# Attention of the first block by pairs of heads, in ten passes a layer instead of 28

## The reference, cut to what matters

```python
proj = h @ w_in                                   # q, k, v (24 heads x 64) and 3 x 1024 gate columns
gates = jax.nn.sigmoid(proj[..., 3 * MIX_WIDTH:]).reshape(B, S, N_BRANCHES, D)
o_a = dilated_mixture(q[:, a_sl], k[:, a_sl], v[:, a_sl])      # 12 heads, 3 groups of 4, merged by logsumexp
o_b = moba_attention(q[:, b_sl], k[:, b_sl], v[:, b_sl])       # 6 heads, one block: causal softmax
o_c = stick_breaking_attention(q[:, c_sl], k[:, c_sl], v[:, c_sl])   # 6 heads, suffix sums of log_sigmoid
y_a = flat(o_a) @ w_out_a                         # likewise y_b, y_c
merged = gates[:, :, 0] * y_a + gates[:, :, 1] * y_b + gates[:, :, 2] * y_c
x = x + merged @ w_o
```

## Time and profile before

| | |
|---|---|
| median of 3 runs | 1539.34 us (1539.24 to 1539.76) |
| span of the profiled execution | 1537.9 us |
| median less span | 1.4 us |
| attention stage of layer 0 (first scores to first `out` product) | 120.05 to 253.60, 133.55 us |
| attention stage of layer 1 | 604.20 to 737.24, 133.04 us |
| first merge by DVE to last, layer 0 | 256.09 to 282.71 us |
| busy in the span | PE 97%, DVE 60%, ACT 52% |

### The profile page before, as it was taken

One profiled execution on the slowest core, in us unless ns is written; L12 is line 12 of the kernel. 1 busy time (PEld: TensorE's weight loads), 2 busy tenths in 40 slices (PEclk: granted clock), 3 DMA queues, 4 the chain that ended last, 5 costly groups with the idle time before them and its releaser, 6 DMA issues.

```text
span 1537.9 us, 21514 instructions
## 1 busy us (share of the span) xinstructions
PE 1484.8 (97%) x8288; PEld 1195.1 (78%) x8288; DVE 918.7 (60%) x1687; ACT 793.9 (52%) x1349; POOL 91.4 (6%) x142
## 2 busy tenths in 40 slices
PE   7999998999999999998999999999999899999998
PEld 6887777799887787877789978787776348788776
DVE  4554456766554554455866666677544874669655
ACT  5445786355534445687445554434565302344774
POOL 6050000000000000000000000000000000041220
PEclk9999999999999999999999999999999999999999
DMA  8782334788554754232489654462222001164200
GB/s 275 253 184 83 125 122 164 219 224 215 192 191 164 276 198 155 83 122 98 171 242 261 191 192 165 164 165 68 71 83 74 22 0 39 45 178 134 81 29 29
DMA packets 183701, 220.96 MB, mean 144 GB/s; under 512 B 6619, under 2 KB 103429, under 8 KB 183600
## 3 DMA queue, kind: packets, MB, share of 16 engines
q1 hardware_dynamic: 179376, 211.65, 43.5%
q0 software_dynamic: 3184, 7.93, 2.6%
q10 hardware_dynamic: 1040, 0.00, 0.0%
HBM read 216.55 MB, written 3.01 MB: 143 GB/s over the span
## 4 chain that ended last, share of the span: by engine, by line
PE 78%; DVE 13%; ACT 6%; issue 3%; DMA 0%; DVEq 0%; SPq 0%; ACTq 0%
PE bank L620 21%; PE bank L622 21%; PE bank L621 21%; DVE w_low L1793 2%; PE bank L1107 2%; ACT w_high L1357 1%; PE bank L863 1%; PE bank L1070 1%; PE bank L704 1%; PE bank L807 1%; PE bank L1083 1%; PE bank L838 1%; PE bank L637 1%; PE bank L812 1%; DVE arena L2150 1%
## 5 line engine op out<-in xcount | busy, mean ns | idle before, releaser
L1793 DVE TENSOR_TENSOR w_low<-raw,w_high 128x1024 fp32r<-128x1024 f32 x344 | 414.9, 1213 | 340.8 <-ACT w_high L1357 335.7
L1357 ACT ACTIVATE w_high<-raw 128x1024 fp32r<-128x1024 f32 x352 | 367.0, 1047 | 334.8 <-PE bank L622 284.8
L620 PE MATMUL bank<-w_high,acts_r 128*128 128x512 f32 (+1 forms) x848 | 339.0, 400 | 11.6 <-DVE w_low L1793 4.9
L621 PE MATMUL bank<-w_low,acts_r 128*128 128x512 f32 (+1 forms) x848 | 329.7, 389 | 0.0
L622 PE MATMUL bank<-w_high,acts_r 128*128 128x512 f32 (+1 forms) x848 | 329.7, 389 | 0.0
L620 PE MATMUL bank<-acts_r,w_high 128*128 128x256 f32 (+1 forms) x736 | 228.9, 311 | 1.5 <-DVE arena L2209 1.3
L622 PE MATMUL bank<-acts_r,w_low 128*128 128x256 f32 (+1 forms) x736 | 225.6, 307 | 0.0
L621 PE MATMUL bank<-acts_r,w_high 128*128 128x256 f32 (+1 forms) x736 | 225.6, 307 | 0.0
L620 PEld LDWEIGHTS bank<-w_high,acts_r 128*128 128x128 f32 x848 | 160.2, 189 | 53.5 <-DVE w_low L1793 6.6
L622 PEld LDWEIGHTS bank<-w_high,acts_r 128*128 128x128 f32 x848 | 159.4, 188 | 36.4
L621 PEld LDWEIGHTS bank<-w_low,acts_r 128*128 128x128 f32 x848 | 159.8, 188 | 32.0
(11 more groups left out here) (315 smaller groups left out, 1789.6 us busy)
## 6 DMA issues: line engine op xcount, KB each, us to landing
raw<-in_w_in SPq DMA_DIRECT2D x69, 1024.0 KB, 5.2
raw<-in_w_up SPq DMA_DIRECT2D x64, 512.0 KB, 6.7
raw<-in_w_down SPq DMA_DIRECT2D x32, 1024.0 KB, 4.9
raw<-in_w_ada SPq DMA_DIRECT2D x24, 1024.0 KB, 6.9
raw<-in_w_in SPq DMA_DIRECT2D x34, 512.0 KB, 5.1
raw<-in_w_o SPq DMA_DIRECT2D x8, 1024.0 KB, 7.6
raw<-in_w_out SPq DMA_DIRECT2D x8, 1024.0 KB, 4.9
raw<-in_w_out_c SPq DMA_DIRECT2D x4, 768.0 KB, 5.3
```

Source lines behind the costliest of these rows:

```text
L620: mm(o, lh, rh, start=start, stop=False)
L621: mm(o, lh, rl, start=False, stop=False)
L1357: run(A_(high, src, ACT.Copy), (high_ready, n + 1))
L1793: run(V.tensor_tensor(low, src, high.bitcast(F32), ALU.subtract), split_done(n))
```

## The change

A unit becomes a pair of heads: A has 2 pairs x 2 tiles, B 3 pairs with both query tiles, C 3 pairs, so ten units, and PE does pass i as `scores(i)`, `second(i - 1)`, `steps_of` filler steps (8, 9, 8, 9, then 10 three times, 9 three times, the last five at the end), `values(i - 1)`. The two heads of a pair alternate: scores on row halves 0 to 63 and 64 to 127, each in its own bank; values with v stationary on column halves, so that the output comes by features and 128 probabilities' columns move. The sums' inverses are spread over the features by a matmul, as in block 2; ACT copies that to `spread1` and DVE multiplies it into `o_feat`. The 16 transposes are gone; `oT` is split per branch, A and B inside the passes (`take_heads_high`, `take_heads_low`). The copy of a gate group by ACT is replaced by a minimum on DVE (`gate_floor`), for which ACT's Abs waits; the four ACT steps of a group are no longer spread over passes. Half of the copies to `PT` go to DVE. The filler's order in a slab is by two k for each tile (`by_tile`).

On PE:

```diff
-                for u in range(len(U) + 2):
-                    if u < len(U):
-                        scores(u)
-                    if 1 <= u <= len(U):
-                        second(u - 1)
-                    advance(filler, 1000 if u >= len(U) else 3 if U[u][0] == "A" else 4)
-                    if u >= 2:
-                        values(u - 2)
-                for b in range(4):
-                    o = open_bank("oT", l, b)
-                    for m in range(4):
-                        ins = tr(o[:, m * P:(m + 1) * P], o_tok[:, t, k * P:(k + 1) * P], ident[:, :])
+                steps_of = {"A": (8, 9), "B": (10,), "C": (9,)}
+                for i in range(len(U) + 1):
+                    if i < len(U):
+                        scores(i)
+                    if i:
+                        second(i - 1)
+                    advance(filler, steps_of[U[i][0]][U[i][2]] if i < len(U) else 1000)
+                    if i:
+                        values(i - 1)
...
+                def scores(i):
+                    if kind == "A" and t:
+                        third = open_bank("s2", l, i, among=ATTENTION_BANKS)
+                        ins = mm(third[:, SEQ:2 * SEQ], head(0, hd, slice(P, SEQ)), head(1, hd, keys), start=True, stop=True)
+                    o = [open_bank("s", l, i, side, among=ATTENTION_BANKS) for side in range(2)]
+                    if kind == "A":
+                        for g in range(G_A - t):
+                            for side in range(2):
+                                ins = mm(o[side][:, g * span:(g + 1) * span], head(0, hd, slice(t * P, (t + 1) * P)),
+                                         head(1, hd, slice(0, span)), start=True, stop=True)
+                        if t:
+                            pe.wait_ge(*third_scored.at(l, i))
+                            ins = mm(third[:, 0:SEQ], head(0, hd, slice(P, SEQ)), head(1, hd, keys), start=True, stop=True)
...
+                def second(i):
+                    for side in range(2):
+                        pe.wait_ge(*probs_ready.at(l, i, side))
+                        o = open_bank("p", l, i, side, among=ATTENTION_BANKS)
+                        for b in range(min(4, blocks)):
+                            ins = tr(o[:, b * P:(b + 1) * P], S[:, i % 2, side, b * P:(b + 1) * P], ident[:, :])
+                    if blocks > 4:
+                        o = open_bank("p", l, i, 2, among=ATTENTION_BANKS)
+                        for side in range(2):
+                            for b in range(4, blocks):
+                                ins = tr(o[:, at_b:at_b + P], S[:, i % 2, side, b * P:(b + 1) * P], ident[:, :])
...
+                    half = [o[side * DH:(side + 1) * DH, :] for side in range(2)]
+                        for b in range(blocks):
+                            for side in range(2):
+                                mm(half[side][:, 0:P], v(g * N_A + 2 * p + side, jt), PT[side][:, b * P:(b + 1) * P],
+                                   start=b == 0, stop=b == blocks - 1)
+                    if kind != "C":
+                        for tt in range(n):
+                            for side in range(2):
+                                inverse = stat[:, (2 * i + side) % 4, 3, tt:tt + 1].to_broadcast([P, DH])
+                                ins = mm(half[side][:, (n + tt) * P:(n + tt + 1) * P], inverse, ident[:, :], start=True, stop=True)
```

On ACT:

```diff
+                def gate_log_steps(key):
+                    splits.due(*key)
+                    if n >= 2:
+                        act.wait_ge(*gate_exponent.at(l, n - 2))
+                    act.wait_ge(*gate_floored.at(l, n))
+                    run(A_(x, bank(*key)[:, :], ACT.Abs, scale=nstat[:, 2, t:t + 1]), emptied(*key))
+                    run(A_(x, x, ACT.Exp, scale=-1.0))
+                    run(A_(x, x, ACT.Ln, bias=eps_col[:, 1:2]), gate_logged.by(l, n))
+                for i in range(len(U) + 1):
+                    if i >= 2:
+                        take_sums(i - 2)
+                    if i:
+                        take_second(i - 1)
+                    if i < len(U):
+                        exponents_of(i)
+                        splits.due("s", l, i, 1)
+                    while len(done) < len(logged):
+                        gate_exp_step()
+                    if i in (6, 9):
+                        take_heads_high((6, 9).index(i))
+                    for key in ended_in[(l, i)]:
+                        gate_log_steps(key)
+                splits.due("o", l, len(U) - 1)
+                take_sums(len(U) - 1)
+                take_heads_high(2)
+                while len(done) < len(logged):
+                    gate_exp_step()
```

On DVE:

```diff
+                def gate_floor(key):
+                    splits.due(*key)
+                    dve.wait_ge(*filled(*key))
+                    run(V.tensor_scalar(g, bank(*key)[:, :], nstat[:, 2, t:t + 1], 0.0, ALU.mult, ALU.min), gate_floored.by(l, len(floored) - 1))
+                for i in range(len(U) + 1):
+                    if i:
+                        invert_sums(i - 1)
+                    early = i >= 2 and U[i - 2][0] == "A"
+                    if early:
+                        take_values(i - 2)
+                    if i < len(U):
+                        maximum(i)
+                    if i >= 2 and not early:
+                        take_values(i - 2)
+                    if i:
+                        take_second(i - 1)
+                    gate_exponents()
+                    if i in (7, 10):
+                        take_heads_low((7, 10).index(i))
+                    if i < len(U):
+                        splits.due("s", l, i, 1)
+                        stick_sums(i)
+                    for key in ended_in[(l, i)]:
+                        gate_floor(key)
+                splits.due("o", l, len(U) - 1)
+                take_heads_low(2)
+                gate_exponents()
```

More of the change, by code:

```diff
@@ L658, in tokens_by_features @@
                 order = [(k, t) for k in range(KD) for t in tiles]
+                if by_tile:
+                    order = [(k, t) for k0 in range(0, KD, 2) for t in tiles for k in (k0, k0 + 1)]
                 if apart:
@@ L798, in scores @@
                     if kind == "A":
                         span = (t + 1) * P
[L800 to L807, removed]
@@ L1428, in take_second @@
                     if kind == "C":
[L1430 to L1431 removed]
+                        for side in range(2):
+                            act.wait_ge(*emptied("p", l, i, side))
+                            run(A_(PT[side][:, 0:384], S[:, i % 2, side, 384:768], ACT.Exp), stick_weights.by(l, i, side))
                         return
[L1433 removed]
@@ new lines, in exponents_of @@
+                def exponents_of(i):
+                    kind, p, t = U[i]
+                    for side in range(2):
+                        st = stat[:, (2 * i + side) % 4, :, :]
+                        s = S[:, i % 2, side, :]
+                        if kind == "C":
+                            act.wait_ge(*emptied("s", l, i, side))
+                            part = s[:, 384:768]
+                            run(A_(part, s[:, 0:384], ACT.Abs))
+                            run.settle()
+                            run(A_(part, part, ACT.Exp, scale=-1.0))
+                            run.settle()
+                            run(A_(part, part, ACT.Ln, bias=eps_col[:, 1:2]), softplus_part.by(l, i, side))
+                            continue
+                        act.wait_ge(*bias_ready.at(l, i))
+                        if kind == "A":
+                            w = blocks_of_pair(kind, t) * P
+                            run(A_(s[:, 0:w], s[:, 0:w], ACT.Exp, bias=st[:, 1, 0:1], scale=SCALE, accum_out=st[:, 2, 0:1]),
+                                probs_ready.by(l, i, side))
+                        else:
+                            for tt in range(TILES):
+                                x = s[:, tt * P:tt * P + (tt + 1) * P]
+                                run(A_(x, x, ACT.Exp, bias=st[:, 1, tt:tt + 1], scale=SCALE, accum_out=st[:, 2, tt:tt + 1]),
+                                    probs_ready.by(l, i, side) if tt else None)
@@ L1509, in _ @@
-                while len(done) < len(copied):
-                    if len(logs) < len(copied):
-                        gate_log_step()
-                    gate_exp_step()
-                for b in range(4):
-                    splits.due("oT", l, b)
-                    act.wait_ge(*filled("oT", l, b))
-                    take_high(A_(oT[:, 0, 2 * b:2 * b + 2, :], bank("oT", l, b)[:, :].rearrange("p (a n) -> p a n", a=2), ACT.Copy),
-                              "oT", l, b)
+                    run(A_(logged[n], logged[n], ACT.Exp), gates_ready.by(l, n))
```

428 lines of the change are left out of this document (209 added, 219 removed).

## The result

The changed kernel takes 1549.14 us (1548.01 to 1549.54), against 1539.76 us for the kernel before in the same series: ratio 1.0057, 95% interval 1.0044 to 1.0071. (Ratios are taken over all fast executions of both kernels and so aren't the quotient of the two medians.) The forecast was 1552.5. So it is slower, a little less than forecast, and that the size came so near is luck: layer 0 lost 10.0 us and layer 1 lost 1.35, where 6.6 each was forecast, and the two errors nearly cancel.

A forecast was written before the change was run, and what follows sets the result against it. PE's order of work bounds the kernel, except where PE stands behind DVE. Tail 3.4 and clock 3.2 us, twice, add 13.2 to the span of 1537.9: 1551.1, plus 1.4 to the median: 1552.5 us; range 1520 to 1566.

The forecast's parts named there:

- PE's work: Attention stage: PE relieved of 21 us a layer, 104 left; a pair of 256-column scores takes 0.45 to 0.50 us.
- that rival: Scores: row halves do not overlap, costing 11.5 us more a layer; 1560 to 1575 us, chance 0.06.
- ACT and DVE: Attention stage: ACT about 86 us, DVE about 80, neither a bound by its sum; order within a pass counts.
- the mechanism that the prediction named: Gate passes: DVE does low parts, then minima; ACT waits for the minimum before 2 x 2.05 us of logarithms.
- Waits in the passes: Attention passes worked: PE waits 26 us in a layer, nearly all of the 21 us given back.
- The clock: Half clock after idle gaps: two losses of 1.6 us a layer, 3.2; bounds none and four (6.4).
- the prediction's use of it: Skill's clock rule: waits of passes 2, 4, 5 and 10 each lose clock, 6.4 us a layer, giving 1558.9.
- the prediction's one place of agreement: Earlier trace: after windows with PE busy 1.46 of 3 us, the clock was 0.50 for the next 3 us.
- The term of +3.4: Tail behind the last gate: first merge at 142.3 against 136.04, DVE done 3.4 us later, same in both layers.
- first merge some 10 us behind the first `out` product: Sign in the trace after, start of `out`: first merge some 10 us behind PE's first product instead of 2.5.
- Neither half nor all of the gain: Rival, PE stays the bound, faster: all waits vanish, 1494 us, or half, 1520; together 0.24, full gain a third.
- No change: Rival: with 3.4 us less a layer and no clock loss the stage comes out even, 1536.3 to 1542.4; 0.13.

The follow-up runs named there:

- e6_copy: Changed kernel with layer 0's conditioning steps moved into pass 1, ACT copying gate groups again and the minimum back in DVE's last step: 1515.14 us.
- e7_all: Changed kernel with conditioning early, minima ahead of low parts, high parts ahead of exponentials and gate logarithms a pass later: 1496.31 us.
- e1_cond: Changed kernel with DVE's three conditioning instructions of layer 0 moved from behind the last gate exponents into pass 1: 1539.82 us.
- e2_floor: Changed kernel with conditioning early, and DVE's gate minima ahead of the low parts due with the gate's bank: 1522.47 us.
- e10_copy_only: Changed kernel with only DVE's minimum undone: ACT copies the gate group again, conditioning stays late: 1530.79 us.
- e5_by_side: Changed kernel with a pair's scores not alternating, all of side 0 and then all of side 1: 1553.74 us.

## Why the prediction was right, and where it wasn't

**PE's work: right.** Six scores of 256 columns in row halves start at 153.03 and the transposes at 154.53: 1.50, so 0.50 for a pair, the upper end of what was taken.

```profile
153.03 0.48 PE L814 MATMUL bank<-arena 64*128 64x256 f32 x1
...
154.53 0.87 PE L866 MATMUL bank<-ident,arena 128*128 128x128 f32 x6
```

Row halves do overlap (before, three heads took that time); that rival falls. The third groups, which the forecast had standing alone (1.95 for the six), overlap with the others too. Values took 1.36 for 24 records, 0.11 a matmul, a spread 0.32. In sum 103.96 us were measured where PE had its full clock, against 104 predicted.

**ACT and DVE: right.** ACT 89.0 and DVE 73.9 us in layer 0 (predicted 86 and 80), 81.7 and 69.1 in layer 1, none a bound by its sum. DVE's minimum takes 0.745 us (predicted 0.68):

```profile
L2076 DVE TENSOR_SCALAR arena<-bank,nstat 128x512 f32<-128x512 f32 x12 | 8.4, 745 | 0.0
```
```profile
L1527 ACT ACTIVATE arena<-bank,nstat 128x512 f32<-128x512 f32 x12 | 8.1, 678 | 15.0 <-DVE arena L2076 15.0
```

ACT stood 15.0 us behind it, the mechanism that the prediction named and e6_copy confirms.

**Waits in the passes: right in place, too large.** By hand against measured: pass 2 4.4 and 3.66, pass 3 0.9 and 0.67, pass 4 3.65 and 3.04, pass 5 5.4 and 4.1, pass 6 1.6 and 0.7, pass 8 5.6 and 3.6, pass 10 4.2 and 1.2; 26 and 17 in sum.

**The clock: right in kind, too small.** The passes began at 8.3, 18.1, 33.9, 44.5, 60.2, 74.8, 85.7, 94.8, 109.8 and 120.1, near to the hand's, though the waits are 9 us shorter. PE's own work makes up the rest. It is busy 112.61 us, 8.65 more than at full clock in e7_all; 1.7 of it in the conditioning matmuls, 7 in the passes, where the forecast had 3.2 and 6.4 as its bound. So the clock's term was some 4 us too small, and the waits 9 us too large. Pass 2, timeline of PE:

```profile
142.84 1.11 PE L873 MATMUL bank<-ident,arena 128*128 128x128 f32 x4 [3.66 <-DVE arena L2060]
143.60 0.78 PE L629 MATMUL bank<-w_high,acts_r 128*128 128x512 f32 x1
...
147.59 0.57 PE L629 MATMUL bank<-w_high,acts_r 128*128 128x512 f32 x1
```

Nine products take 3.99 us, 0.42 to 0.58 each, instead of 0.23. The same pass takes 15.8 us here and 9.6 without the wait in e7_all: a wait of 3.66 cost 6.2 (in layer 1, where the pass takes 15.0, it cost 5.4). So taking waits away can bring more than their sum. For e6_copy it can be counted: from e1_cond the stage up to the first `out` product shrank from 129.88 to 117.61 us, 7.5 of it the listed waits (19.6 to 12.1), 4.8 PE's busy time (110.16 to 105.39). The Trainium skill (TensorE: Matmul & The Clock Gate, HAM oscillation) has this loss behind longer idle gaps. By the prediction's use of it, 6.4 a layer, the size is nearly right. Its places were not: half clock followed the waits of passes 2 and 4 and the wait of 1.8 us at the end of pass 8, and not those of pass 5 (2.1 and 2.0) and 10 (1.2). A fall behind 1.8 us is not what that section has, and the measurement decides. Nor was the prediction's one place of agreement a longer gap: PE stood there 1.12, 0.94 and 0.92 us, with work between.

**The step that failed: the tail of layer 0.** The prediction took layer 0 and layer 1 as equal ("Layer 1 has the same order, +3.4"). It had listed DVE's order behind the last gate and left out its three steps on `cond`, which stand in the program behind `gate_exponents()` in layer 0 alone, and for which PE's conditioning product waits, ahead of `out`. Before, DVE had done them 1.0 us ahead of PE's product, and they cost nothing, but the trace before has both rows (DVE, then PE):

```profile
250.48 0.18 DVE L2009 TENSOR_TENSOR cond<-cond,cond_e 128x16 f32<-128x16 f32 x1
```
```profile
251.67 1.92 PE L704 MATMUL bank<-raw,cond 128*32 128x512 f32 x16
```

The term of +3.4 for layer 0's last merge, +6.6 with the clock, was +10.0; e1_cond puts 8 to 9 us on this wait. With it the sign "first merge some 10 us behind the first `out` product" failed in layer 0 (3.6 us; 8.3 in layer 1). Layer 1's +6.6 was +1.35: its first merge is 2.4 us sooner than by hand, which is mostly pass 10, where the wait on `stick_sums` was 3.0 shorter, and the 3.2 of clock added on top was already in the passes' times.

**The rivals.** Neither half nor all of the gain came, but e7_all shows that the mechanism given for it was sound: first merge at 116.0 behind the stage's start, where it had said 116. "No change" is what e1_cond gives, so the forecast was right by a wait that it didn't know: that the kernel came out slower at all is, for the prediction, luck.

## What to carry to other kernels

When PE is relieved, read what stands behind ACT and DVE at each place of their program, not their sums: here four reorderings that remove no work turned 1549 us into 1496. List every instruction behind the last piece of a stage, the ones done only in the first layer too; three of 0.6 us in all held PE for 11 here, because of what stood ahead of them. Price a wait of PE above its own length where PE then runs at half clock.

## What the hardware showed beyond expectation

**A similar wait cost a clock change or none.** Windows of 3 us around the wait of pass 2, changed kernel and then e6_copy, PEclk third from last:

```profile
140.00:143.00 3.00, 0.16 (x1) 0.17 (x2) 0.51 (x2) 2.88 (x6) 0.00 (x0) 0.69 0.32 122
143.00:146.00 3.00, 3.00 (x10) 2.52 (x11) 2.70 (x8) 2.01 (x7) 0.00 (x0) 0.50 0.00 0
```
```profile
140.00:143.00 3.00, 1.35 (x8) 1.23 (x9) 1.66 (x7) 2.38 (x7) 0.00 (x0) 1.00 0.35 134
143.00:146.00 3.00, 3.00 (x14) 2.40 (x14) 2.38 (x4) 3.00 (x8) 0.00 (x0) 1.00 0.00 0
```

A wait of 3.66 us brought 1.2 GHz, one of 2.37 kept 2.4 GHz, though PE was busy 1.35 of 3 us; in the earlier trace rows 1.46 of 3 was followed by 0.50, and at the end of pass 8 a wait of 1.76 was. The plainest case is one kernel, e2_floor: its wait of pass 2 is 2.55 us in layer 0 and 2.54 in layer 1, and the 3 us behind it are

```profile
143.00:146.00 3.00, 2.88 (x9) 2.49 (x10) 2.96 (x9) 1.96 (x7) 0.00 (x0) 0.50 0.01 3
618.65:621.65 3.00, 2.88 (x15) 2.43 (x16) 2.96 (x9) 2.41 (x8) 0.00 (x0) 1.00 0.02 5
```

The pass takes 13.9 us in layer 0 and 12.4 in layer 1. So the traces give no rule by the length of the wait alone. How this bears on the spread of a kernel's executions stays open: e10_copy_only went from 1524.0 to 1533.3 us, with clocks of 0.985 to 0.992, but the changed kernel, in which the clock fell several times, only from 1548.0 to 1549.5.

**Row halves overlap without strict alternation.** With two heads of one half issued ahead of two of the other, 256-column scores took the same time (e5_by_side: 1.50 us for the six of pass 3, as in the changed kernel). With three and three, the six of 128 columns in pass 2 took 1.19 us instead of 0.87.
